# Pick 12 of every expert unit is gathered in two bounded halves

## The chip, the cores and the metric

The kernel runs on one core of a Trainium2 chip. The metric is the device time of one launch in microseconds (us). Engines are named as the profile names them: PE is TensorE (matrix products), PEld its weight loads, DVE is VectorE, ACT is ScalarE, POOL is GpSimd, SP is SyncE. POOL issues the indirect DMAs (gathers), SP the plain loads of weights. The gathers run on DMA queue q0, SP's loads on q1, and all queues share the core's 16 DMA engines.

## What is computed

The reference is a small model over 256 tokens of width 1024: two layers of attention with feed-forward blocks, then a state-space layer and a windowed attention layer, each followed by an expert layer ("peer") and a gated addition ("ple"). The change touches the two expert layers alone. Cut to what matters, one such layer is:

```
def peer_ffn(x, norm_g, q_w, sub_keys, u, v):
    h = rmsnorm(x, norm_g).reshape(T, D)                       # T = 256 tokens, D = 1024
    q = (h @ q_w).reshape(T, PEER_HEADS, 2, PEER_HALF)         # 8 heads
    s = einsum('thcd,ckd->thck', q, sub_keys)                  # 2 x 128 key scores per token and head
    s1, i1 = top_k(s[:, :, 0], 16)
    s2, i2 = top_k(s[:, :, 1], 16)
    ... the best 16 of the 256 sums s1 + s2; idx = i1 * 128 + i2, one of 16384 experts
    gate = softmax(best_s)
    a = einsum('nd,nhkd->nhk', h, u[idx])
    w = gate * gelu(a)
    out = einsum('nhk,nhkd->nd', w, v[idx])
```

So each token picks 16 experts per head, 128 in all, and for each of them a row of `u` and a row of `v` is fetched and used once.

## The kernel before

Everything is in 32-bit floats. The tokens are two blocks of 128, one token on each of 128 partitions. An expert's `u` and `v` rows lie side by side in one table in HBM, `experts`, of 2 x 16384 rows (both layers, one behind the other) of 2048 floats, which is 8 KB. One gather is one indirect DMA: it reads a row number from each partition and fetches that row, 128 rows or 1.05 MB in all.

**Units and picks.** A unit is one head of one token block: 16 units per layer (n = 0 to 15), 16 picks each (k = 0 to 15), so 256 gathers per layer and 512 in the kernel. Pick g of the kernel goes to buffer `held[g % 11]`; there are 11 buffers (`HELD`). Each buffer has its semaphore `expert_landed[g % 11]`, which a gather raises by 16 when it has landed.

**Who does what to a pick.** POOL waits until the buffer is free (`expert_free`, raised by PE after the pick that had the buffer before) and issues the gather (`gather` in `expert_rows`, L2840). DVE waits for the landing and multiplies the `u` half by the token's row, summing it to `a` (`dots`, L2723). ACT makes GELU, the weight, and a diagonal matrix of weights per pick (`weights`, L1903 to L1912). PE multiplies the diagonal with the `v` half in two products of 512 columns, each issued as more than one MATMUL record (`values`, L1300 and L1303), summing all picks of a block in PSUM. Picks are handled in order and in groups: 4 groups of 4 in units 0 to 14 (`EVEN`); in unit 15 (`FINE`) groups of two up to (12, 13), then 14 alone, then 15 alone. ACT starts on a group when DVE has finished all of its picks.

**What stands between.** In unit n DVE does, in this order: the dots of group 0, the gates, the top 16 keys of unit n+1 (`top_keys`, L2665 and on), the dots of group 1, the best pairs of unit n+1 (`top_pairs`), the dots of group 2, the expert numbers of unit n+1 (`experts_of`, L2179 to L2190), the dots of group 3. The last instruction of `experts_of_picks` (L2190) raises `peer_idx`, for which POOL waits before it issues pick 0 of unit n+1. In units 0 to 5, PE puts one more product of queries (L1258, with the key scores L1288) ahead of groups 0 and 2, and `top_keys` needs those scores, which ACT copies out (L1884).

**Behind the last unit.** When pick 255 is summed, DVE adds the result to the token rows (L2228), PE transposes them (L594) and works through the gate products of the ple layer (L695 to L697). The weight blocks of those products come by SP's loads; SP holds the fifth of them back until pick 253 of the layer (k = 13 of unit 15) has landed (`HELD_BACK`), and the others follow it.

Of the kernel before, what the change touches and what calls it, by code (L numbers as in the profile page):

```python
# [31 lines left out]
KEYS = 128  # L32
# [102 lines left out]
PICKS = UNITS * TOPK  # L135
HELD = 11
HELD_AT = 8088
SPACE = 31808
QUERY = {AT[f"peer{l}_q"] + m: (l, m) for l in range(2) for m in range(SUBS)}
NEXT_IN_RING = {AT[f"peer{l}_q"] + SUBS + i: AT[f"peer{l}_q"] + SLOTS + i for l in range(2) for i in range(RING)}  # L140
OUTS = {AT["ssm_out"]: 0, AT["swa_out"]: 1}
HELD_BACK = {AT[f"ple{l}_gate"] + 4: PICKS * (l + 1) - 3 for l in range(2)}
LAST_GATES = {AT[f"ple{l}_gate"] + 4 + i: PICKS * (l + 1) - HELD + i for l in range(2) for i in range(4)}
# [14 lines left out]
def build_program(nc, stream, experts, x_in, pos_in, cols_in, rows_in, out):  # L158
    n_blocks = AT["end"]
    ctx = ExitStack()  # L160
    with ctx:
# [149 lines left out]
        def peer_regions():  # L311
            r = places(ARENA, ("own", (2 * KEYS,)), ("s", (TB, SUBS, KEYS)), ("s2", (2, KEYS)), ("sv", (2, TOPK)),
                       ("si", (2, TOPK)), ("cand", (256,)), ("cand2", (256,)), ("bs", (TOPK,)),
                       ("bp", (TOPK,)), ("pa", (2, TOPK)), ("pf", (2, TOPK)), ("eq", (2, TOPK, TOPK)),
                       ("pk", (2, TOPK)), ("at", (TOPK,)), ("idx", (2, TOPK)), ("e", (2, TOPK)), ("sum", (1,)),
                       ("rc", (1,)), ("gate", (2, TOPK)), ("a", (2, TOPK)), ("g", (2, TOPK)), ("w", (2, TOPK)),
                       limit=HELD_AT)
            r["held"], _ = region(HELD_AT, HELD, EXPERT)
            r["q0"] = r["cand"]
            r["diag"] = split(row[:, 1, :], 2 * GROUP, P)  # L320
            r["qT"] = pick[:, 0:2, :]
            return r
# [191 lines left out]
        def _(sp):  # L514
# [6 lines left out]
            while b < n_blocks:  # L521
# [40 lines left out]
                    end += 1  # L562
                if b in HELD_BACK:
                    pick_of = HELD_BACK[b]
                    sp.wait_ge(expert_landed[pick_of % HELD], 16 * (pick_of // HELD + 1))
                first = b - RING + 1 if way == "used" else SPLIT[b - RING][2] + 1
                free = used if way == "used" else lo_ready[way]
                turns = (end - b) // RING
# [1454 lines left out]
        def _(dve):  # L2023
# [149 lines left out]
            def experts_of_picks(l, n, first, end):  # L2173

                R = peer_regions()
                si, bp, pa = R["si"].bitcast(U32), R["bp"].bitcast(U32)[:, first:end], R["pa"].bitcast(U32)
                wide, bits = (8, 3) if (first, end) == (0, 8) else (TOPK, 4)
                ks = slice(first, end)
                dve.tensor_scalar(pa[:, 0, ks], bp, bits, None, ALU.logical_shift_right)  # L2179
                link(dve.tensor_scalar(pa[:, 1, ks], bp, wide - 1, None, ALU.bitwise_and))  # L2180
                link(dve.tensor_copy(R["pf"][:, :, ks], pa[:, :, ks]))
                full = [P, 2, end - first, wide]
                eq = R["eq"][:, :, ks, 0:wide]
                iota = col("iota")[:, 0:wide].unsqueeze(1).unsqueeze(1).to_broadcast(full)
                link(dve.tensor_tensor(eq, R["pf"][:, :, ks].unsqueeze(3).to_broadcast(full), iota, ALU.is_equal))
                link(dve.tensor_tensor(eq, eq, si[:, :, 0:wide].unsqueeze(2).to_broadcast(full), ALU.mult))
                link(dve.tensor_reduce(R["pk"][:, :, ks].unsqueeze(3), eq, AX.X, ALU.add))
                link(dve.scalar_tensor_tensor(R["at"][:, ks], R["pk"][:, 0, ks], float(KEYS), R["pk"][:, 1, ks],
                                              ALU.mult, ALU.add))
                return dve.tensor_scalar(R["idx"].bitcast(U32)[:, n % 2, ks], R["at"][:, ks], float(KEYS * KEYS * l), None,  # L2190
                                         ALU.add)

            def add(n, y):

# [483 lines left out]
            def peer(l):  # L2678
# [38 lines left out]
                def dots(n, group):  # L2717
                    h = bank(4 + 2 * (n // PH), 2)
                    for k in range(*groups_of(n)[group]):
                        g = PICKS * l + TOPK * n + k  # L2720
                        u = R["held"][:, g % HELD, 0:D]
                        dve.wait_ge(expert_landed[g % HELD], 16 * (g // HELD + 1))
                        last = dve.scalar_tensor_tensor(u, u, 1.0, h, ALU.mult, ALU.mult,  # L2723
                                                        accum_out=R["a"][:, n % 2, k:k + 1])
                    last.then_inc(of("peer_a"), 1)
# [84 lines left out]
        def _(pool):  # L2810
# [19 lines left out]
            def expert_rows(l, at):  # L2830
                R = peer_regions()
                base = AT[f"peer{l}_q"]
                idx = R["idx"].bitcast(U32)

                def gather(n, ks):
                    for k in ks:
                        g = PICKS * l + TOPK * n + k
                        if g >= HELD:
                            pool.wait_ge(of("expert_free"), g - HELD + 1)
                        pool.indirect_dma_start(R["held"][:, g % HELD, :], None, experts,  # L2840
                                                bass.IndirectOffsetOnAxis(ap=idx[:, n % 2, k:k + 1], axis=0))\
                            .then_inc(expert_landed[g % HELD], 16)

                pool.wait_ge(of("peer_idx0"), l + 1)
# [182 lines left out]
```

## Time and profile before

| | |
|---|---|
| time, median of 3 runs | 2739.67 us (2739.56 to 2741.49) |
| span of the profiled execution | 2739.2 us |
| PE busy | 2461.3 us (90%) |
| DVE busy | 1915.0 us (70%) |
| ACT busy | 1178.3 us (43%) |
| POOL busy | 855.8 us (31%) |
| gathers (POOL DMA_INDIRECT) | 512, first issued at 1265.4 us, last at 2691.2 us |

The span runs from the first to the last instruction; the timed runs are 0.4 to 2.3 us above it. The busy shares are means over stages that have different limits: the two expert layers lie at about 1265 to 1930 us and 2050 to 2715 us, and the shares of the page say little of them. A row of the timeline has the start, the length, the engine, the line, the operation, output and inputs, and in brackets how long the engine was idle before it and who ended that.

### The profile page before, as it was taken

The page shows a single profiled execution, that of the slowest core. Times are in us where ns is not written, and L with a number is a line of the kernel's source. Part 1 is how long each engine was busy: PE and PEld are TensorE (multiplying, and loading weights), DVE is VectorE, ACT ScalarE, POOL GpSimd, SP SyncE. Part 2 cuts the span into 40 slices and gives each one's busy share as a digit, 9 for nine tenths or more (in the row PEclk, how much of TensorE's full clock was granted, in tenths as well). Part 3 has the DMA queues.
Part 4 walks back from the last instruction along what each step waited for, and adds up shares of the span by engine and source line. Part 5 has one row for each costly group of instructions (what it writes and reads, how often), then busy time and mean ns, then how long its engine had stood idle before and what let it go on. Part 6 is the DMA issues. An engine that isn't in the chain of part 4 may idle for free.

```text
span 2739.2 us, 32208 instructions
## 1 busy us (share of the span) xinstructions
PE 2461.3 (90%) x10416; PEld 1678.3 (61%) x10416; DVE 1915.0 (70%) x3841; ACT 1178.3 (43%) x2586; POOL 855.8 (31%) x700
## 2 busy tenths in 40 slices
PE   8999999999989999998998787789988998777688
PEld 7888788888778877986544333334765454333244
DVE  7885588888768875654676767666667676776675
ACT  4446744444564456563333333333453333323334
POOL 0005400000230026754333333444433333333442
PEclk9999999999999999999999889999999999999999
DMA  6654365556425553448999999999639999999996
GB/s 209 189 180 139 117 198 190 172 192 190 158 70 195 188 163 127 165 142 331 420 418 421 417 419 415 414 414 420 205 142 413 420 421 421 417 420 417 411 414 265
DMA packets 142240, 783.39 MB, mean 286 GB/s; under 512 B 15904, under 2 KB 16416, under 8 KB 76576
## 3 DMA queue, kind: packets, MB, share of 16 engines
q0 software_dynamic: 73728, 536.90, 47.4%
q1 hardware_dynamic: 65648, 237.45, 26.1%
q10 hardware_dynamic: 2736, 7.46, 0.9%
q8 instruction: 66, 1.08, 0.2%
q14 instruction: 62, 0.51, 0.1%
HBM read 780.69 MB, written 1.05 MB: 285 GB/s over the span
## 4 chain that ended last, share of the span: by engine, by line
PE 48%; DMA 22%; issue 9%; DVE 8%; ACT 7%; POOL 6%; another core or an unknown queue 0%; POOLq 0%; ACTq 0%; SPq 0%; DVEq 0%
DMA arena<-experts,arena 22%; PE ps L717 11%; PE ps L1300 6%; PE ps L1303 6%; PE ps L718 6%; PE ps L695 5%; PE ps L696 5%; PE ps L697 5%; POOL ring_lo L401 4%; DVE arena L2723 2%; ACT row L1912 2%; POOL arena L2840 1%; PE ps L1258 1%; ACT arena L1905 1%; ACT L1903 1%
## 5 line engine op out<-in xcount | busy, mean ns | idle before, releaser
L2723 DVE SCALAR_TENSOR_TENSOR arena<-arena,ps 128x1024 f32<-128x1024 f32 x512 | 616.4, 1219 | 370.3 <-DMA arena<-experts,arena 354.0
L1300 PE MATMUL ps<-arena,row 128*128 128x512 f32 x1024 | 568.3, 638 | 197.3 <-ACT row L1912 190.3
L2840 POOL DMA_INDIRECT arena<-experts,arena x512 | 485.3, 948 | 761.4 <-PE ps L1303 508.9
L1303 PE MATMUL ps<-arena,row 128*128 128x512 f32 x1024 | 549.7, 620 | 0.0
L717 PE MATMUL ps<-hT,ring_hi 128*128 128x512 f32 x1408 | 503.4, 400 | 2.9 <-DVE hT L2239 2.7
L394 ACT ACTIVATE ring_hi<-ring 128x1024 fp32r<-128x1024 f32 x408 | 429.8, 1058 | 172.4 <-PE ps L697 127.4
L1300 PEld LDWEIGHTS ps<-arena,row 128*128 128x128 f32 x1024 | 198.2, 202 | 474.5 <-ACT row L1912 259.5
L401 POOL TENSOR_TENSOR ring_lo<-ring,ring_hi 128x1024 fp32r<-128x1024 f32 x139 | 334.5, 2416 | 235.0 <-ACT ring_hi L394 212.7
L718 PE MATMUL ps<-hT,ring_lo 128*128 128x256 f32 x1408 | 395.9, 281 | 0.0
L1303 PEld LDWEIGHTS ps<-arena,row 128*128 128x128 f32 x1024 | 205.5, 201 | 266.4 <-issue 266.4
L401 DVE TENSOR_TENSOR ring_lo<-ring,ring_hi 128x1024 fp32r<-128x1024 f32 x269 | 324.1, 1228 | 18.3 <-ACT ring_hi L394 17.6
L717 PEld LDWEIGHTS ps<-hT,ring_hi 128*128 128x128 f32 x1408 | 265.3, 188 | 69.7 <-issue 3.1
L2817 POOL TENSOR_TENSOR rs<-ms,cols 128x1 f32<-128x1 f32 (+1 forms) x41 | 26.4, 645 | 842.2 <-DVE ms L2053 733.1
L718 PEld LDWEIGHTS ps<-hT,ring_lo 128*128 128x128 f32 x1408 | 266.7, 189 | 2.8
L1903 ACT ACTIVATE arena<-arena 128x4 f32<-128x4 f32 (+1 forms) x138 | 28.4, 206 | 533.2 <-DVE arena L2723 513.3
L1912 ACT ACTIVATE row<-cols,arena 128x128 f32<-128x128 f32 x512 | 164.6, 390 | 4.5
L695 PE MATMUL ps<-ring_hi,w 128*128 128x512 f32 x352 | 138.3, 393 | 3.0 <-DVE ring_lo L401 3.0
L1542 ACT ACTIVATE arena<-arena 128x256 f32<-128x256 f32 x88 | 36.9, 419 | 235.7 <-DVE arena L2280 235.7
L696 PE MATMUL ps<-ring_lo,w 128*128 128x512 f32 x352 | 137.9, 392 | 0.0
L697 PE MATMUL ps<-ring_hi,w 128*128 128x512 f32 x352 | 137.0, 389 | 0.0
L695 PE MATMUL ps<-hT,ring_hi 128*128 128x256 f32 (+1 forms) x392 | 114.1, 291 | 4.3 <-POOL ring_lo L401 2.4
L1905 ACT ACTIVATE arena<-arena 128x1 f32<-128x1 f32 x512 | 110.2, 284 | 4.5
(350 smaller groups left out, 3599.4 us busy)
## 6 DMA issues: line engine op xcount, KB each, us to landing
ring<-stream SPq DMA_DIRECT2D x424, 512.0 KB
arena<-experts,arena POOLq DMA_INDIRECT x512
row<-rows_in ACTq DMA_DIRECT2D x11, 512.0 KB, 5.2
arena<-stream SPq DMA_DIRECT2D x8, 512.0 KB, 5.8
queries_in_ring_hi<-stream SPq DMA_DIRECT2D x8, 512.0 KB
queries_in_w<-stream SPq DMA_DIRECT2D x4, 512.0 KB, 7.8
queries_in_h_lo<-stream SPq DMA_DIRECT2D x4, 512.0 KB, 5.3
x<-x_in SPq DMA_DIRECT2D x1, 1024.0 KB, 5.3
```

Source lines behind the costliest of these rows:

```text
L394: act.activation(part(b)[0], raw(b), ACT.Copy).then_inc(hi_ready, 1)
L401: e.tensor_tensor(lo, raw(b), hi.bitcast(F32), ALU.subtract).then_inc(lo_ready[who], 1)
L695: pe.matmul(dst, a[0], b[0], start=start, stop=False)
L696: pe.matmul(dst, a[0], b[1], start=False, stop=False)
L697: return pe.matmul(dst, a[1], b[0], start=False, stop=stop)
L717: pe.matmul(ps[:, bank_at, :], hi, hT[:, :, k, :], start=k == 0, stop=False)
L718: last = pe.matmul(ps[:, bank_at, 0:T], lo, hT_hi[:, k, :], start=False, stop=k == KD - 1)
L1300: lower = pe.matmul(ps[:, 2 * tb, :], diag, v[:, 0:HALF], start=first, stop=end)
L1303: pe.matmul(ps[:, 2 * tb + 1, :], diag, v[:, HALF:D], start=first, stop=end)\
L1912: last = act.activation(R["diag"][:, k % (2 * GROUP), :], col("ident"), ACT.Copy, scale=R["w"][:, n % 2, k:k + 1])
L2723: last = dve.scalar_tensor_tensor(u, u, 1.0, h, ALU.mult, ALU.mult, accum_out=R["a"][:, n % 2, k:k + 1])
L2840: pool.indirect_dma_start(R["held"][:, g % HELD, :], None, experts, bass.IndirectOffsetOnAxis(ap=idx[:, n % 2, k:k + 1], axis=0))\
```

## The change

Pick 12 of each unit is gathered by two indirect DMAs into its one buffer. The first takes the same row numbers as before, but has an upper bound, the last row of the lower half of the layer's table (8192 of 16384 rows); partitions whose number is above are left out. The second takes a second list of numbers, `upper`, in which a number of the lower half has been raised by 2^20, so that it is beyond its bound (the end of the table) and is left out. DVE makes that list with two more instructions on one column per unit. The second DMA is issued after pick 15 of the unit, and ahead of it POOL waits until the first has landed. Both raise the buffer's semaphore by 16, and `landed(g)` counts what to wait for.

```diff
+EXTRA_AT = HELD_AT + HELD * EXPERT
+IN_TWO = 12
+LOWER = 8192
+OUT_OF_RANGE = float(1 << 20)
...
+def landed(g):
+
+    return 16 * sum(1 + (h % TOPK == IN_TWO) for h in range(g % HELD, g + 1, HELD))
...
                     pick_of = HELD_BACK[b]
-                    sp.wait_ge(expert_landed[pick_of % HELD], 16 * (pick_of // HELD + 1))
+                    sp.wait_ge(expert_landed[pick_of % HELD], landed(pick_of))
...
-                return dve.tensor_scalar(R["idx"].bitcast(U32)[:, n % 2, ks], R["at"][:, ks], float(KEYS * KEYS * l), None,
-                                         ALU.add)
+                base = float(KEYS * KEYS * l)
+                if end == TOPK:
+                    late = slice(IN_TWO, IN_TWO + 1)
+                    link(dve.tensor_scalar(R["past"][:, late], R["at"][:, late], float(LOWER), OUT_OF_RANGE, ALU.is_lt, ALU.mult))
+                    dve.scalar_tensor_tensor(R["upper"].bitcast(U32)[:, n % 2, late], R["past"][:, late], base, R["at"][:, late],
+                                             ALU.add, ALU.add)
+                return dve.tensor_scalar(R["idx"].bitcast(U32)[:, n % 2, ks], R["at"][:, ks], base, None, ALU.add)
...
-                        dve.wait_ge(expert_landed[g % HELD], 16 * (g // HELD + 1))
+                        dve.wait_ge(expert_landed[g % HELD], landed(g))
...
+                        into = R["held"][:, g % HELD, :]
+                        if k != IN_TWO:
+                            pool.indirect_dma_start(into, None, experts,
+                                                    bass.IndirectOffsetOnAxis(ap=idx[:, n % 2, k:k + 1], axis=0))\
+                                .then_inc(expert_landed[g % HELD], 16)
+                            continue
+                        pool.indirect_dma_start(into, None, experts,
+                                                bass.IndirectOffsetOnAxis(ap=idx[:, n % 2, k:k + 1], axis=0),
+                                                bounds_check=KEYS * KEYS * l + LOWER - 1, oob_is_err=False)\
+                            .then_inc(expert_landed[g % HELD], 16)
+                    if IN_TWO in ks:
+                        g = PICKS * l + TOPK * n + IN_TWO
+                        pool.wait_ge(expert_landed[g % HELD], landed(g) - 16)
                         pool.indirect_dma_start(R["held"][:, g % HELD, :], None, experts,
-                                                bass.IndirectOffsetOnAxis(ap=idx[:, n % 2, k:k + 1], axis=0))\
+                                                bass.IndirectOffsetOnAxis(ap=upper[:, n % 2, IN_TWO:IN_TWO + 1], axis=0),
+                                                bounds_check=2 * KEYS * KEYS - 1, oob_is_err=False)\
                             .then_inc(expert_landed[g % HELD], 16)
```

On POOL, from the first gathers of the first expert layer to the start of unit 1, the program before has these rows (picks 0 to 7 and a small power, picks 8 to 10, picks 11 to 15, pick 0 of unit 1, the rest of unit 1):

```order
L2840 DMA arena<-experts,arena 128x2048 [waits blocks_used,peer_idx0]
L2840 DMA arena<-experts,arena 128x2048 x7
L2817 TENSOR_TENSOR rs<-ms,cols 128x1 [waits ms_ready]
L2840 DMA arena<-experts,arena 128x2048 [waits peer_idx]
L2840 DMA arena<-experts,arena 128x2048 x2
L2840 DMA arena<-experts,arena 128x2048 [waits expert_free] x5
L2840 DMA arena<-experts,arena 128x2048 [waits expert_free,peer_idx]
L2840 DMA arena<-experts,arena 128x2048 [waits expert_free] x15
```

The changed program has in the same place, from the small power on (L2864 is the bounded first gather of pick 12, L2871 the second):

```order
L2835 TENSOR_TENSOR rs<-ms,cols 128x1 [waits ms_ready]
L2860 DMA arena<-experts,arena 128x2048 [waits peer_idx]
L2860 DMA arena<-experts,arena 128x2048 x2
L2860 DMA arena<-experts,arena 128x2048 [waits expert_free]
L2864 DMA arena<-experts,arena 128x2048 [waits expert_free]
L2860 DMA arena<-experts,arena 128x2048 [waits expert_free] x3
L2871 DMA arena<-experts,arena 128x2048 [waits expert_landed1]
L2860 DMA arena<-experts,arena 128x2048 [waits expert_free,peer_idx]
L2860 DMA arena<-experts,arena 128x2048 [waits expert_free] x11
```

The second gather of pick 12 stands behind picks 13, 14 and 15, waits for the first to land, and pick 0 of the next unit stands behind it.

On DVE, in unit 0 of the first expert layer, the step that makes the expert numbers of unit 1 reads before, from the dot of pick 11 to that of pick 12:

```order
L2723 SCALAR_TENSOR_TENSOR arena<-arena,ps 128x1024 [waits expert_landed0]
L2179 TENSOR_SCALAR arena<-arena 128x16
L2180 TENSOR_SCALAR arena<-arena 128x16
L2181 CAST arena<-arena 128x32 [waits dve_chain]
L2185 TENSOR_TENSOR arena<-arena,cols 128x512 [waits dve_chain]
L2186 TENSOR_TENSOR arena<-arena 128x512 [waits dve_chain]
L2187 TENSOR_REDUCE arena<-arena 128x32 [waits dve_chain]
L2188 SCALAR_TENSOR_TENSOR arena<-arena 128x16 [waits dve_chain]
L2190 TENSOR_SCALAR arena<-arena 128x16 [waits dve_chain]
L2723 SCALAR_TENSOR_TENSOR arena<-arena,ps 128x1024 [waits expert_landed1]
```

and in the changed program its second half reads:

```order
L2200 TENSOR_REDUCE arena<-arena 128x32 [waits dve_chain]
L2201 SCALAR_TENSOR_TENSOR arena<-arena 128x16 [waits dve_chain]
L2206 TENSOR_SCALAR arena<-arena 128x1 [waits dve_chain]
L2207 SCALAR_TENSOR_TENSOR arena<-arena 128x1 [waits dve_chain]
L2209 TENSOR_SCALAR arena<-arena 128x16
L2741 SCALAR_TENSOR_TENSOR arena<-arena,ps 128x1024 [waits expert_landed1]
```

Two one-column instructions, L2206 and L2207, stand ahead of the one that releases POOL (L2209 now, L2190 before). The order of the dots is the same.

## Rows read from the trace of the kernel before

**Rows 1.** Page, part 3: DMA queue, kind: packets, MB, share of 16 engines.

```profile
q0 software_dynamic: 73728, 536.90, 47.4%
```

**Rows 2.** Windows: us; PE, PEld, DVE, ACT, POOL busy; clock; DMA share; GB/s.

```profile
1280.00:1915.00 635.00, 540.65 (x1332) 256.70 (x1330) 436.99 (x1068) 214.25 (x676) 246.61 (x253) 0.94 1.01 418
2070.00:2698.00 628.00, 527.86 (x1308) 249.64 (x1307) 434.97 (x1062) 212.81 (x670) 247.26 (x252) 0.95 1.01 417
```

**Rows 3.** Waits from 1280 to 1925 us: total, times, longest.

```profile
DVE arena L2723 <- DMA arena<-experts,arena: 183.2, 153, 2.6
...
POOL arena L2840 <- PE ps L1303: 256.8, 156, 14.0
POOL arena L2840 <- DVE arena L2190: 93.7, 14, 8.1
```

**Rows 4.** Timeline of POOL, units 3 and 4 of the first expert layer.

```profile
1421.83 0.94 POOL L2840 DMA_INDIRECT arena<-experts,arena  x1 [0.78 <-PE ps L1303]
1430.90 0.94 POOL L2840 DMA_INDIRECT arena<-experts,arena  x1 [8.14 <-DVE arena L2190]
```

**Rows 5.** Timeline of DVE, units 3 and 4 of the first expert layer.

```profile
1425.98 1.22 DVE L2723 SCALAR_TENSOR_TENSOR arena<-arena,ps 128x1024 f32<-128x1024 f32 x1 [1.26 <-DMA arena<-experts,arena]
...
1430.01 0.17 DVE L2190 TENSOR_SCALAR arena<-arena 128x16 uint32<-128x16 f32 x1
1430.10 1.21 DVE L2723 SCALAR_TENSOR_TENSOR arena<-arena,ps 128x1024 f32<-128x1024 f32 x1
...
1431.24 1.22 DVE L2723 SCALAR_TENSOR_TENSOR arena<-arena,ps 128x1024 f32<-128x1024 f32 x1
...
1435.91 1.22 DVE L2723 SCALAR_TENSOR_TENSOR arena<-arena,ps 128x1024 f32<-128x1024 f32 x1 [1.25 <-DMA arena<-experts,arena]
...
1438.40 1.22 DVE L2723 SCALAR_TENSOR_TENSOR arena<-arena,ps 128x1024 f32<-128x1024 f32 x1 [1.25 <-DMA arena<-experts,arena]
```

**Rows 6.** Timeline of ACT and DVE at the start of unit 3's key search.

```profile
1408.32 0.63 ACT L1884 ACTIVATE arena<-ps,rs 128x128 f32<-128x128 f32 x2 [7.84 <-PE ps L1288]
...
1408.97 0.49 DVE L2665 MAX8 arena<-arena 128x8 f32<-128x128 f32 x2 [1.97 <-ACT arena L1884]
```

**Rows 7.** Timeline of DVE, last picks (13, 14, 15) of the first expert layer.

```profile
1917.61 1.22 DVE L2723 SCALAR_TENSOR_TENSOR arena<-arena,ps 128x1024 f32<-128x1024 f32 x1 [1.26 <-DMA arena<-experts,arena]
...
1920.10 1.22 DVE L2723 SCALAR_TENSOR_TENSOR arena<-arena,ps 128x1024 f32<-128x1024 f32 x1 [1.25 <-DMA arena<-experts,arena]
...
1923.25 1.22 DVE L2723 SCALAR_TENSOR_TENSOR arena<-arena,ps 128x1024 f32<-128x1024 f32 x1 [1.92 <-DMA arena<-experts,arena]
```

**Rows 8.** Timeline of PE, last picks of the first expert layer.

```profile
1918.08 1.02 PE L1303 MATMUL ps<-arena,row 128*128 128x512 f32 x2
1920.37 1.13 PE L1300 MATMUL ps<-arena,row 128*128 128x512 f32 x2 [1.27 <-ACT row L1912]
...
1927.44 0.66 PE L594 MATMUL ps<-cols,x 128*128 128x128 f32 x4
```

**Rows 9.** Timeline, same place in the second expert layer (DVE: picks 13, 15).

```profile
2702.83 1.22 DVE L2723 SCALAR_TENSOR_TENSOR arena<-arena,ps 128x1024 f32<-128x1024 f32 x1 [2.23 <-DMA arena<-experts,arena]
...
2705.59 1.13 PE L1300 MATMUL ps<-arena,row 128*128 128x512 f32 x2 [2.24 <-ACT row L1912]
...
2708.42 1.22 DVE L2723 SCALAR_TENSOR_TENSOR arena<-arena,ps 128x1024 f32<-128x1024 f32 x1 [1.87 <-DMA arena<-experts,arena]
```

**Rows 10.** Timeline of PE in unit 13 of the first expert layer, after an idle stretch.

```profile
1812.11 1.02 PE L1303 MATMUL ps<-arena,row 128*128 128x512 f32 x2
1817.85 2.08 PE L1300 MATMUL ps<-arena,row 128*128 128x512 f32 x2 [4.72 <-ACT row L1912]
...
1824.13 1.02 PE L1300 MATMUL ps<-arena,row 128*128 128x512 f32 x2
```

**Rows 11.** Window inside that stretch, columns as in rows 2.

```profile
1818.00:1822.00 4.00, 4.00 (x5) 1.71 (x6) 2.40 (x6) 0.00 (x0) 0.09 (x1) 0.50 1.02 424
```

**Rows 12.** Timeline of SP, the held-back weight loads.

```profile
1917.61 41.45 SPq L579 DMA_DIRECT2D ring<-stream  x12
```

More of the change, by code:

```diff
@@ L318, in peer_regions @@
             r["held"], _ = region(HELD_AT, HELD, EXPERT)
+            r["upper"], at = region(EXTRA_AT, 2, TOPK)
+            r["past"], at = region(at, TOPK)
             r["q0"] = r["cand"]
@@ L2832, in expert_rows @@
                 base = AT[f"peer{l}_q"]
-                idx = R["idx"].bitcast(U32)
+                idx, upper = R["idx"].bitcast(U32), R["upper"].bitcast(U32)
                 def gather(n, ks):
```

## The prediction

> **What bounds the kernel now.** I read the page for the queues, then windows over the two gather stages, then the waits in them, then the timelines around one unit and around the last picks of a layer. The gathers bring 536.90 MB over q0 [rows 1], 512 of 1.05 MB each. In both stages the 16 DMA engines are busy all the time (share 1.01) and move 417 to 418 GB/s [rows 2], which is 2.5 us per gather. DVE, the first user of a pick, waits for landings 183.2 us in 153 places of the first stage [rows 3], and the dots of picks that it waits for start 2.49 us apart (1917.61, 1920.10) [rows 7]. So the rate of the DMA engines sets the length of a stage, as long as the queue never runs dry; POOL, DVE, ACT and PE have slack inside it. POOL's 256.8 us of waiting for PE and 93.7 us for L2190 [rows 3] are waiting for free buffers and for the next unit's numbers, with gathers queued meanwhile. How many: pick 15 of unit 3 is issued at 1421.83 and its dot starts at 1435.91, 14.1 us or five to six gathers later; pick 0 of unit 4 is issued at 1430.90 and used at 1438.40, 7.5 us or three gathers later [rows 4, 5]. The second is the thinnest point.
>
> At the end of a layer the bound changes: the last landing is followed by a chain through DVE, ACT and PE with nothing beside it. The dot of pick 13 starts at 1917.61 [rows 7], and the diagonals of the group (12, 13) let PE start at 1920.37, 2.76 us later. PE then works without a gap through picks 12 to 15 until the transposes at 1927.44 [rows 8]. The last dot, at 1923.25 [rows 7], is not in that chain, since pick 15's products stand behind three other picks'. The second layer repeats it (2702.83 to 2705.59, also 2.76 us; last dot at 2708.42) [rows 9].
>
> **Bytes and queue.** If left-out rows are not moved, each pick 12 still brings 128 rows, and the stage moves the same bytes. Thirty-two more indirect DMAs add only their own start and end. The rows show no fixed part per gather when the queue is full: 1.05 MB at 418 GB/s takes 2.51 us, the spacing of the dots 2.49 us. I take 0 for the 32. The other end is a left-out row that takes the time of a moved one: a second full gather per unit, 32 x 2.49 = 80 us. No row shows a bounded gather; I take the end where the row is simply absent.
>
> **The wait on POOL.** Behind it stand only pick 0 of the next unit and what follows. The first half of pick 12 lands before pick 13, and in unit 3 pick 11's dot starts at 1425.98 [rows 5]; half a gather later is 1427.2, a whole one 1428.5 at the worst division of the rows over the engines. POOL issues the second half then, 0.94 us, and is done by 1429.5, while the release for pick 0 comes with L2190 at 1430.01 and the issue at 1430.90 [rows 4, 5]. Picks 13 to 15 are in the queue meanwhile, 7.5 us of work. So the wait is covered by DVE's making of the numbers, at 0 us; a bounded gather could take about 1.4 us longer than 0.94 on POOL before it shows, and then pick 0 still has its own queue cover. That cover is 7.5 less its own transfer of 2.49, so at most 5.0 us, less whatever start the DMA needs; I take 2 us as safe. DVE's two instructions delay L2190 by 0.17 us each and a gap, 0.4 us together [rows 5]: 0 under that cover, 32 x 0.4 = 13 us without it.
>
> **The order of landing.** The second half of pick 12 is queued behind pick 15, so pick 12 is complete about when pick 15 was before. DVE takes dots in order, so in each unit the dots of 12 to 15 start together there. In unit 3 that is 1435.91 instead of 1430.10. At 1.14 us a dot (1430.10 to 1431.24) they end 4 x 1.14 later, 3.4 us after the end of pick 15's dot before. Next unit's picks come every 2.49 us from 1438.40 [rows 5], so DVE gains 1.35 us per pick and is level at its third. PE gets the group 3.4 us late and frees buffers 3.4 us late, which costs 1.4 of the five to six gathers queued there. In units 0 to 5 the lateness also reaches the key search, which already waits 1.97 us for scores made behind that group [rows 6]; it has the landing of four more picks, 10 us, to recover before the numbers are due. Inside the stage I put 0, with bounds of 0 and 2 us in each of the six such units of a layer, 24 us.
>
> **The end of a layer.** Here nothing covers the lateness. With the last bytes landing as before, the dot of pick 12 starts at 1923.25, that of 13 1.14 us later at 1924.39, and PE starts the group 2.76 us after that, at 1927.15 instead of 1920.37: 6.8 us later. In the second layer 2708.42 + 1.14 + 2.76 = 2712.32 instead of 2705.59: 6.7 us. PE then has the same four picks to do.
>
> Two things come on top. PE ends the group before at about 1919 [rows 8] and would now be idle for 8 us. After 4.72 us of idleness in unit 13 the next picks ran at a granted clock of 0.50, the level of 1.2 GHz [rows 10, 11]: from 1817.85 to 1824.13, 6.28 us, for eight MATMUL records that take 8 x 0.43 = 3.4 us at the pace of the layer's end (sixteen from 1920.37 to 1927.3) [rows 8]. So up to 2.8 us; the trace has shorter such stretches too, and I take 2.0. And SP's held-back loads start when pick 13 has landed (1917.61) [rows 12]; with only half of pick 12 ahead of it that is 1.2 us earlier, while more of the gathers is still to come. Before, the last dot came 3.15 instead of 2.49 us after the one ahead of it, 0.7 us of sharing; with half a gather more to share I take 0.5 us more. What follows the transposes is PE's own chain and moves as a whole.
>
> **Sum.** Per layer 6.8 + 2.0 + 0.5 = 9.3 us, two layers 18.6 us, inside the stages 0. Against the profiled span of 2739.2 that is 2757.8; the median of the runs shown is 0.5 above the span, so 2758.3 us, 0.7% slower. This case's own range is 2750 (no clock loss, no sharing, 2 x 6 us less a little) to 2768 (full clock loss, some of the units' bounds).
>
> **Rivals.**
> *Starved units.* The late group and the late numbers empty the queue in units 0 to 5. For it speaks the wait in [rows 6] and the three gathers of cover at pick 0; against it that four landings lie between. Up to 24 us more, or with 13 us for the DVE instructions 37 more: 2765 to 2795. Chance 0.15.
> *Left-out rows cost as moved ones, or a part of it.* Nothing in the trace speaks for or against; full price 80 + 18.6 makes 2838, half price 2798. Chance 0.06.
> *Each gather pays a fixed part.* If the engines finish one gather before the next, a half costs more than half. From the rows, the most that one can hide is the 5.0 us between issue and transfer of pick 0, 160 us for 32; against it stands the 2.49 us spacing, which leaves nothing. Should a fifth of it show, 2790. Chance 0.04. The Trainium skill, DMA: Bandwidth & Descriptors, on the anatomy of one DMA of the GpSimd path, puts a fixed cost of about 2.0 us on each DMA; by that, 32 more would be an estimated 64 us, were none overlapped. This trace does not show it between queued gathers (2.49 us apart).
> *POOL is slow on a bounded gather.* Sixty-four of them. Up to 2.3 us each nothing shows; at 10 us each, the excess over the cover of 3.4 us is 6 us in 30 units: 2930. Chance 0.04; a mild form falls in the first rival.
> *Not slower.* The end of a layer is set by the gate weights and not by PE: SP's loads start 1.2 us earlier, and if the gate products had to wait for them, PE's lateness would be hidden: 2737 to 2742. This decides only if those products now waited at least 9 us for weights, but PE goes from the last pick to the transposes without a stop [rows 8] and the loads start 10 us before. Chance 0.06.
>
> **Numbers.** The forecast has 0.65. Its 2758 is the prediction; 2747 to 2788 leaves out the costly left-out rows, slow POOL, fixed parts, the worst starvation and no change, about 0.2 together. A difference under 0.2% (5.5 us) cannot be told from none here. Slower is the forecast, the starved units and the three costly rivals, less a margin for a smaller end: 0.91. Same 0.06, faster 0.03.
>
> **What the profile would show.** Queue q0: the same megabytes, 32 x 16 more packets; more megabytes would be the second rival. In a unit, four dots of picks 12 to 15 back to back 1.14 us apart, after one wait for a landing, and POOL's L2871 issued ahead of the release by DVE. DMA share still 1.0 and the stages 635 and 628 us long within 2 us. At a layer's end, PE idle for some 8 us ahead of its last four picks and a granted clock of 0.5 behind that. Wrong would be the sum if the share fell inside the stages, if POOL's instruction grew past 2 us, or if the gates took up the lateness.

## The result and the profile after

The changed kernel takes 2766.32 us (median of 4 runs, 2765.81 to 2767.43), the kernel before on the same chip 2740.35 (4 runs, 2739.56 to 2741.49): ratio 1.0093, 95% interval 1.0082 to 1.0105, 26.0 us slower. The forecast was 18.6 us more than the profiled span and 2758 us in all; the time lies inside the range. The profiled span grew from 2739.2 to 2764.3 us, by 25.1.

First the page, part 1, part 3 (queue: packets, MB, share of 16 engines) and part 6 (issues, us to landing), of the kernel after:

```profile
span 2764.3 us, 32368 instructions
PE 2471.7 (89%) x10416; PEld 1681.3 (61%) x10416; DVE 1923.5 (70%) x3905; ACT 1177.1 (43%) x2586; POOL 892.8 (32%) x732
...
q0 software_dynamic: 78336, 536.92, 47.2%
...
HBM read 814.25 MB, written 1.05 MB: 295 GB/s over the span
...
arena<-experts,arena POOLq DMA_INDIRECT x544, 10.6
```

The queue carries the same megabytes as in [rows 1], with 4608 packets more: 512 for the 32 added DMAs (16 each) and 4096, which is one for each row left out (32 times 128). The counter of HBM reads was 780.69 MB before and is 33.56 MB higher, 4096 rows of 8 KB: it counts the rows left out in full. Whether the time does is for the experiments.

The windows of [rows 2], of the kernel after:

```profile
1280.00:1915.00 635.00, 525.61 (x1285) 248.20 (x1284) 440.61 (x1096) 212.14 (x669) 263.51 (x267) 0.93 1.01 415
2070.00:2698.00 628.00, 523.17 (x1270) 247.96 (x1270) 438.13 (x1103) 209.01 (x658) 263.15 (x267) 0.92 1.01 415
```

The DMA share is still 1.01, but the rate is 415 instead of 418 and 417 GB/s, 0.5 to 0.7% less: in 635 us some 3 to 5 us of gathers. So something was lost inside the stages too. The waits of the first stage (1280 to 1925 us; total, times, longest), of DVE and POOL:

```profile
DVE arena L2741 <- DMA arena<-experts,arena: 159.3, 86, 6.8
DVE arena L2683 <- ACT arena L1897: 25.4, 5, 6.1
...
POOL arena L2860 <- PE ps L1316: 243.9, 130, 9.3
POOL arena L2871 <- DMA arena<-experts,arena: 44.8, 12, 6.3
...
POOL arena L2860 <- DVE arena L2209: 23.3, 14, 2.6
```

POOL's wait for the next unit's numbers went from 93.7 us [rows 3] to 23.3, because POOL now stands at L2871 for most of that time. Grown is the second row: DVE's key search waits 25.4 us for the scores that ACT copies out. In the kernel before, the same view has for it:

```profile
DVE arena L2665 <- ACT arena L1884: 8.1, 4, 5.6
```

Around pick 0 of unit 4, the place of [rows 4, 5], the timelines of POOL and DVE after are:

```profile
1422.39 1.00 POOL L2864 DMA_INDIRECT arena<-experts,arena  x1 [1.31 <-PE ps L1316]
...
1429.66 1.50 POOL L2871 DMA_INDIRECT arena<-experts,arena  x1 [1.70 <-DMA arena<-experts,arena]
1432.67 0.94 POOL L2860 DMA_INDIRECT arena<-experts,arena  x1 [1.52 <-DVE arena L2209]
```

```profile
1431.97 0.15 DVE L2206 TENSOR_SCALAR arena<-arena 128x1 f32<-128x1 f32 x1
1432.15 0.16 DVE L2207 SCALAR_TENSOR_TENSOR arena<-arena 128x1 uint32<-128x1 f32 x1
1432.23 0.17 DVE L2209 TENSOR_SCALAR arena<-arena 128x16 uint32<-128x16 f32 x1
1438.50 1.22 DVE L2741 SCALAR_TENSOR_TENSOR arena<-arena,ps 128x1024 f32<-128x1024 f32 x1 [6.10 <-DMA arena<-experts,arena]
...
1439.65 1.22 DVE L2741 SCALAR_TENSOR_TENSOR arena<-arena,ps 128x1024 f32<-128x1024 f32 x1
...
1440.79 1.22 DVE L2741 SCALAR_TENSOR_TENSOR arena<-arena,ps 128x1024 f32<-128x1024 f32 x1
...
1441.93 1.22 DVE L2741 SCALAR_TENSOR_TENSOR arena<-arena,ps 128x1024 f32<-128x1024 f32 x1
```

L2871 is issued before the numbers are ready, and pick 0 still waits for DVE: the added wait is covered. The four dots of picks 12 to 15 run back to back behind one wait. Both are as forecast. L2209 comes 2.2 us later than L2190 did. Of that 0.8 us is the later start of the whole layer (its first gather is issued at 1266.21 instead of 1265.41), 1.2 the lateness of pick 11 of unit 3 counted from there, and 0.2 the two added instructions.

The end of the first layer, DVE (picks 11 to 13) and PE, the place of [rows 7, 8]:

```profile
1917.79 1.22 DVE L2741 SCALAR_TENSOR_TENSOR arena<-arena,ps 128x1024 f32<-128x1024 f32 x1 [1.25 <-DMA arena<-experts,arena]
...
1929.42 1.22 DVE L2741 SCALAR_TENSOR_TENSOR arena<-arena,ps 128x1024 f32<-128x1024 f32 x1 [10.41 <-DMA arena<-experts,arena]
...
1930.57 1.22 DVE L2741 SCALAR_TENSOR_TENSOR arena<-arena,ps 128x1024 f32<-128x1024 f32 x1
```

```profile
1927.92 1.02 PE L1316 MATMUL ps<-arena,row 128*128 128x512 f32 x2
1933.33 1.78 PE L1313 MATMUL ps<-arena,row 128*128 128x512 f32 x2 [4.38 <-ACT row L1925]
1934.90 1.91 PE L1316 MATMUL ps<-arena,row 128*128 128x512 f32 x2
1936.61 1.26 PE L1313 MATMUL ps<-arena,row 128*128 128x512 f32 x2
1937.70 1.02 PE L1316 MATMUL ps<-arena,row 128*128 128x512 f32 x2
...
1942.08 0.66 PE L607 MATMUL ps<-cols,x 128*128 128x128 f32 x4
```

From the dot of pick 13 to PE is 1933.33 - 1930.57 = 2.76 us, as before. PE's first six records then take 4.37 us (1933.33 to 1937.70), where 6 x 0.43 = 2.6 would do, and PE needs 8.75 us to the transposes where it needed 7.07 [rows 8]: 1.7 us for the clock. The window inside that stretch has a granted clock of 0.58, between the two levels, nearer to 1.2 GHz:

```profile
1933.00:1937.00 4.00, 3.67 (x5) 1.63 (x6) 1.08 (x2) 2.90 (x8) 0.89 (x1) 0.58 0.00 0
```

In the second layer PE's wait is 3.77 us, and the record behind it has the full pace (1.12 us, where layer 1 has 1.78):

```profile
2730.93 1.12 PE L1313 MATMUL ps<-arena,row 128*128 128x512 f32 x2 [3.77 <-ACT row L1925]
```

**Where the 25.1 us are.** I take each row's time from the first gather of its layer and set it against the same row of before. That gives four stretches: how late the dot of pick 11 of the last unit is (everything inside the stage), how much later the last landing and the dots of 12 and 13 let PE start, and PE's pace until the transposes.

| us later than before | layer 1 | layer 2 | forecast, a layer |
|---|---|---|---|
| pick 11 of unit 15 (inside the stage) | 4.4 | 3.7 | 0 |
| one dot, then 2.76 us to PE, behind the last landing | 6.8 | 6.7 | 6.8 |
| last landing further behind pick 11 | 1.0 | 0.4 | 0.5 |
| clock | 1.7 | 0.0 | 2.0 |
| PE at the transposes | 13.8 | 10.9 | 9.3 |

That is 24.8 of the 25.1 us. Each number is from one execution of each kernel; the same reading of e1 below, whose gathers are those of before, is up to 1.6 us off at the pick 11 of single units, and 0.4 and 0.1 us at that of unit 15. The third line is, in layer 1, (1929.42 - 1917.79) less what lay before between the dot of pick 11 (1912.64) and that of pick 15 (1923.25): 11.63 - 10.61. In layer 2 PE's pace did not fall. The end of the layer is near what was forecast (9.5 and 7.1 us, for 9.3); the 8.1 us of the first line were put at 0.

**How the late group makes pick 11 late.** Pick 11 of a unit goes into the buffer that pick 0 of the same unit had, so POOL can issue it only when PE has summed that pick 0. Here are its issue (POOL) and its dot (DVE) in unit 4 of layer 1, before:

```profile
1453.89 0.94 POOL L2840 DMA_INDIRECT arena<-experts,arena  x1 [5.92 <-PE ps L1303]
...
1465.73 1.22 DVE L2723 SCALAR_TENSOR_TENSOR arena<-arena,ps 128x1024 f32<-128x1024 f32 x1 [1.22 <-DMA arena<-experts,arena]
```

and after:

```profile
1461.54 0.94 POOL L2860 DMA_INDIRECT arena<-experts,arena  x1 [5.92 <-PE ps L1316]
...
1469.34 1.22 DVE L2741 SCALAR_TENSOR_TENSOR arena<-arena,ps 128x1024 f32<-128x1024 f32 x1
```

Counted from the layer's first gather, the issue is 6.8 us later, and the dot 2.8: before, 11.8 us lay between issue and dot, after 7.8. In units 3, 4 and 5 of layer 1 the issue is 4.4, 6.8 and 8.1 us late, and the time from issue to dot falls from 11.0, 11.8 and 12.8 us to 7.8 in each, so the dot is 1.2, 2.8 and 3.1 us late. The cover here was 3 to 5 us, and it is used up. Pick 0, in contrast, has more of it than before in unit 4 (10.4 us from issue to dot instead of 7.5). The windows from 1464 to 1472 us, before and then after, show that the queue runs short for a moment (share 1.01 and 0.95):

```profile
1464.00:1472.00 8.00, 8.00 (x31) 5.30 (x30) 6.57 (x15) 3.23 (x12) 1.49 (x2) 1.00 1.01 422
```

```profile
1464.00:1472.00 8.00, 8.00 (x20) 3.58 (x19) 7.79 (x21) 1.48 (x6) 4.59 (x5) 1.00 0.95 345
```

So what empties the queue is a buffer that PE frees late, and not the numbers of the next unit.

### The profile page after: what moved, and what is told of

Its sections match the earlier page's. It is cut to its first block, busy times and chain, and to the rows that moved or that the text cites. A ratio compares the mean times of both kernels' runs of the same rounds, so it can differ in the third digit from the quotient of the medians.

```text
span 2764.3 us, 32368 instructions
## 1 busy us (share of the span) xinstructions
PE 2471.7 (89%) x10416; PEld 1681.3 (61%) x10416; DVE 1923.5 (70%) x3905; ACT 1177.1 (43%) x2586; POOL 892.8 (32%) x732
## 3 DMA queue, kind: packets, MB, share of 16 engines
HBM read 814.25 MB, written 1.05 MB: 295 GB/s over the span
## 4 chain that ended last, share of the span: by engine, by line
PE 49%; DMA 21%; DVE 10%; issue 9%; ACT 6%; POOL 5%; POOLq 0%; ACTq 0%; SPq 0%; DVEq 0%
DMA arena<-experts,arena 21%; PE ps L730 11%; PE ps L1313 7%; PE ps L1316 6%; PE ps L731 5%; PE ps L708 5%; PE ps L709 5%; PE ps L710 5%; DVE arena L2741 4%; POOL ring_lo L414 4%; ACT row L1925 2%; ACT arena L1918 1%; ACT L1916 1%; DVE ring_lo L414 1%; DVE arena L2732 1%
## 5 line engine op out<-in xcount | busy, mean ns | idle before, releaser
L2741 DVE SCALAR_TENSOR_TENSOR arena<-arena,ps 128x1024 f32<-128x1024 f32 x512 | 604.5, 1218 | 343.6 <-DMA arena<-experts,arena 342.2
L1313 PE MATMUL ps<-arena,row 128*128 128x512 f32 x1024 | 579.0, 649 | 221.4 <-ACT row L1925 221.4
L2860 POOL DMA_INDIRECT arena<-experts,arena x480 | 453.5, 945 | 597.6 <-PE ps L1316 485.1
L1316 PE MATMUL ps<-arena,row 128*128 128x512 f32 x1024 | 557.2, 627 | 0.0
L1313 PEld LDWEIGHTS ps<-arena,row 128*128 128x128 f32 x1024 | 201.8, 205 | 500.2 <-ACT row L1925 286.0
L1316 PEld LDWEIGHTS ps<-arena,row 128*128 128x128 f32 x1024 | 208.9, 204 | 273.4 <-issue 273.4
```

Source lines behind the costliest of these rows:

```text
L1313: lower = pe.matmul(ps[:, 2 * tb, :], diag, v[:, 0:HALF], start=first, stop=end)
L1316: pe.matmul(ps[:, 2 * tb + 1, :], diag, v[:, HALF:D], start=first, stop=end)\
L2860: pool.indirect_dma_start(into, None, experts, bass.IndirectOffsetOnAxis(ap=idx[:, n % 2, k:k + 1], axis=0))\
```

## The experiments

The theory: landing order alone costs, at two places, the layer's end and the late group inside the stage. The rivals: the DVE instructions, the rows left out, the bounded gather itself, and the wait on POOL. All kernels compute the whole output. Each group of runs shared its runs of the kernel before: 2740.79 us for the first four, 2743.12 for the next four, 2743.49 for the last four; each ratio is against its own group. Where a kernel splits only some of the gathers, this helper replaces the test `k != IN_TWO`, and `landed` counts by it:

```
+def in_two(g):
+    n = g % PICKS // TOPK
+    return g % TOPK == IN_TWO and n == UNITS - 1
```

**e1, the numbers alone** (`n < 0`: the two DVE instructions stay, no gather is split).

> The kernel before with DVE's two instructions for the second list alone; no pick is split. Placing theory (the loss lies at a layer's end and in units 0 to 5, DVE's instructions are covered): 2740 us, within 1. Rival, late numbers: 0.4 us in each of 32 units, 2753.

Measured: 2740.28 us, ratio 0.9995 [0.9985, 1.0004]. The two instructions cost nothing that can be seen (interval -4.1 to +1.1 us).

**e2, the last unit alone** (`n == UNITS - 1`).

> Pick 12 is split in unit 15 of each layer alone. Placing theory: the layer's end is worth 3.4 us of late dots, 3 to 5 us of late and slower PE and about 1 us of queue per layer, 16 us in all: 2756. Rival, every split costs alike (26 us over 32): 2742.

Measured: 2761.77 us, ratio 1.0076 [1.0059, 1.0093], 21.0 us. Two split gathers of 32 (one in each layer) bring four fifths of the loss, 5 us more than the 16 that I expected for them. The timeline of PE at the end of its first layer:

```profile
1927.07 2.08 PE L1319 MATMUL ps<-arena,row 128*128 128x512 f32 x2 [9.37 <-ACT row L1931]
1928.94 1.91 PE L1322 MATMUL ps<-arena,row 128*128 128x512 f32 x2
1930.65 1.52 PE L1319 MATMUL ps<-arena,row 128*128 128x512 f32 x2
1932.00 1.02 PE L1322 MATMUL ps<-arena,row 128*128 128x512 f32 x2
```

PE is idle for 9.37 us (forecast: some 8) and then takes 4.93 us for six records, 2.4 us lost to the clock (forecast: 2.0).

**e3, all units but the last** (`n < UNITS - 1`).

> Pick 12 is split in units 0 to 14, and is whole in unit 15. Placing theory: 3 us per layer from a queue that runs short in the first units, 2746. Rival, every split costs alike: 30 of 32 remain, 2764.

Measured: 2751.59 us, ratio 1.0043 [1.0029, 1.0057], 10.8 us. Splits inside the stage do cost, not nothing as in the forecast, and more than the 6 us expected here. The sum with e2 is 31.8, more than the 26.0 of both together. The trace shows where: of e3's +4.7 us at the transposes of layer 1 only 1.5 are a late last dot. The rest is PE, which has a wait in unit 14,

```profile
1891.60 2.08 PE L1319 MATMUL ps<-arena,row 128*128 128x512 f32 x2 [4.91 <-ACT row L1931]
```

and no idle time from there to the transposes at 1932.17. In the kernel before PE had little idle time there: it was busy from 1880 to 1910 us, and waited for 0.17 and 1.27 us between 1910 us and the transposes. Its window (columns as in [rows 2]) of the kernel before:

```profile
1880.00:1910.00 30.00, 30.00 (x80) 14.90 (x79) 18.96 (x31) 11.54 (x37) 17.74 (x16) 0.98 1.01 420
```

So what PE loses to the late group of unit 14, beyond the little idle time that lay behind it, it carries to the end, unless it must wait there anyway, as in the full change.

**e4, the dot of pick 12 last.** The split stays everywhere; in units 0 to 14 DVE takes 13, 14 and 15 as they land, and 12 behind them.

```
-                    for k in range(*groups_of(n)[group]):
+                    picks = range(*groups_of(n)[group])
+                    for k in (13, 14, 15, 12) if picks == range(12, 16) else picks:
```

> As the changed kernel, but in units 0 to 14 DVE takes the dots of the last group in the order 13, 14, 15, 12, so that one dot and not four follows the late landing. If the late group starves the first units: 3 us per layer come back, 2760. If POOL's wait or the numbers do: no change, 2766.

Measured: 2761.86 us, ratio 1.0075 [1.0058, 1.0091], 21.1 us, which is e2's loss. Pick 11 of unit 15 is 0.8 us late in layer 1 and 1.5 in layer 2, where it was 4.4 and 3.7 in the changed kernel. In no unit does its dot start less than 10 us after its issue, and the window from 1464 to 1472 us has a share of 1.01 again. The waits of its first stage, columns as above:

```profile
DVE arena L2742 <- DMA arena<-experts,arena: 179.0, 154, 2.4
DVE arena L2683 <- ACT arena L1897: 5.2, 4, 2.4
```

With three of the four dots on time the key search waits 5.2 us, not 25.4. So the split gathers, the rows left out and the wait on POOL, all of them still there, cost next to nothing inside a stage (0.8 and 1.5 us here); the order of DVE's dots, and through it the time at which PE gets the group and frees its buffers, cost the rest.

**e5, e6 and e7, the stage in parts** (`n < 6`; `6 <= n < 13`; `13 <= n < 15`).

> Pick 12 is split in units 0 to 5 of each layer alone. Placing theory: here the key search waits behind the late group, so the queue runs short: 2 to 3 us per layer, 2745 (2743 to 2747). If the shortness is spread over all units: 2 us, 2742.

> Pick 12 is split in units 6 to 12 alone. Placing theory: PE has no queries or gates beside the picks there and catches up, the queue stays full: 2740, within 1.5. If every split costs alike (26 us over 32): 11 us, 2751.

> Pick 12 is split in units 13 and 14 alone. Theory from the run without unit 15: PE is full from unit 13 on (gate products beside the picks) and carries the late group of unit 14 to the layer's end, 3 us per layer: 2746. If the loss of that run came from the first units alone: 2740.

Measured: e5 2746.42, ratio 1.0012 [1.0002, 1.0021]; e6 2742.23, 0.9998 [0.9988, 1.0007]; e7 2748.08, 1.0019 [1.0009, 1.0028]. That is +3.3, -0.9 and +5.0 us; the interval of e5 starts at 0.5 us. The units between, in which PE makes no key scores ahead of the groups and which are far from the layer's end, are free. In the waits of its first stage, e5 has the same long stop of the key search as the changed kernel:

```profile
DVE arena L2689 <- ACT arena L1903: 25.6, 5, 6.0
```

In e5 the dot of pick 11 starts 7.8 us after its issue in units 3, 4 and 5 of both layers, in the changed kernel 7.8 to 8.3. In e2, e6 and e7, whose first units are not split, it takes 10 us or more there. In layer 1 of e5 pick 11 is 2.9 us late by unit 5, as in the changed kernel, but the last dot of the layer only 1.7 (layer 1) and -0.2 us (layer 2): where the later units are not split, part of the lateness is given back. By which slack, I did not settle, and the execution in the trace is the shortest of e5's ten (2742.30 us).

**e8, the first gather is whole.** It has no bound and moves all 128 rows; the second leaves all of them out.

```
-   ... R["past"][:, late], R["at"][:, late], float(LOWER), OUT_OF_RANGE, ALU.is_lt, ALU.mult
+   ... R["past"][:, late], R["at"][:, late], float(KEYS * KEYS), OUT_OF_RANGE, ALU.is_lt, ALU.mult
...
-                                               bass.IndirectOffsetOnAxis(ap=idx[:, n % 2, k:k + 1], axis=0),
-                                               bounds_check=KEYS * KEYS * l + LOWER - 1, oob_is_err=False)\
+                                               bass.IndirectOffsetOnAxis(ap=idx[:, n % 2, k:k + 1], axis=0))\
```

> As the changed kernel, but the first gather of pick 12 takes all 128 rows and the second leaves all 128 out; the order and the waits are the same, and so is the number of left-out rows. Order theory: the same landing of pick 12 behind pick 15, 2766 (2763 to 2768); the empty gather itself adds nothing. If the cost were in moving the second half of the rows late (1.2 us of transfer behind pick 15): up to 2.5 us less per layer, 2761.

Measured: 2767.26 us, ratio 1.0082 [1.0065, 1.0098], 24.1 us. It makes no difference how the bytes divide over the two gathers, nor that the second brings none. That leaves the order: DVE must wait for a DMA that is queued behind three others. The sharing with the held-back weights should have been less, with the whole pick moved early; the loss is not smaller beyond the interval. In its profiled execution, the longest of the four, layer 1 ends 11.2 us late and layer 2 15.9. The second number is 5.0 us more than in the changed kernel. Of these 2.9 come inside the stage: pick 11 is 5.4 us late in unit 5 (3.1 in the changed kernel) and 6.6 in unit 15 (3.7). The other 2.1 are PE's pace: after 6.66 us of idleness it takes 9.16 us to the transposes, where it took 7.06. Why the stage loses more there, I do not know.

**e9, empty gathers aside.** The kernel before, with 120 more gathers (one behind each group of units 1 to 15) that leave every row out, into a region that nobody reads.

```
+                        pool.indirect_dma_start(aside, None, experts.rearrange("e (h d) -> (e h) d", h=2),
+                                                bass.IndirectOffsetOnAxis(ap=nowhere[:, 0:1], axis=0),
+                                                bounds_check=4 * KEYS * KEYS - 1, oob_is_err=False)\
+                            .then_inc(of("aside_landed"), 16)
```

> The kernel before, no pick split, with four more gathers in each of units 1 to 15, one behind each group: all their numbers are beyond the bound, so all 128 rows (4 KB each) are left out; they go to unused space, and only the next of them waits for one. 15360 left-out rows, nearly four times those of the change. If a left-out row costs nothing on the DMA engines: 2742 (2739 to 2745). If it costs the reading that the page counts for it: 63 MB at 418 GB/s, 150 us more, 2890.

Measured: 2751.07 us, ratio 1.0028 [1.0017, 1.0039], 7.6 us, more than I expected. Over 120 gathers that is 0.06 us each (0.04 to 0.09 by the interval), with all that such a gather costs on POOL included. The page, part 3, of this kernel:

```profile
q0 software_dynamic: 91008, 536.97, 47.7%
...
HBM read 843.61 MB, written 1.05 MB: 307 GB/s over the span
```

The read counter rose by 62.9 MB, 15360 rows of 4 KB. At the 418 GB/s of [rows 2] such bytes would take 150 us; the kernel lost 7.6. So they are counted, and their time is not paid.

**e10, the wait with an empty queue.** The second half is issued right behind the first, ahead of pick 13, and POOL waits in between, inside its loop over the picks, with no gather behind the first half in the queue.

```
-                    if IN_TWO in ks:
-                        g = PICKS * l + TOPK * n + IN_TWO
                         pool.wait_ge(expert_landed[g % HELD], landed(g) - 16)
                         pool.indirect_dma_start(R["held"][:, g % HELD, :], None, experts,
...
```

> As the changed kernel, but the second half of pick 12 is issued before pick 13, so POOL waits for the first half with nothing queued behind it, and the order of landing is kept. If the three gathers between are what hides the wait: the queue idles about 4.5 us per unit (a half gather takes at least 5.9 us from issue to landing, 1.2 of it transfer), 2885 (2840 to 2920). If POOL's wait is harmless by itself: 2745.

Measured: 2957.88 us, ratio 1.0784 [1.0766, 1.0802], 214 us or 6.7 for each split, above the range that I gave. The timeline of POOL around one such place, and the window of its first stage (the profile names no releaser for this wait; it puts the other 31, 320.9 us, down to the DMA):

```profile
1440.62 1.00 POOL L2864 DMA_INDIRECT arena<-experts,arena  x1 [1.30 <-PE ps L1316]
1451.22 1.37 POOL L2869 DMA_INDIRECT arena<-experts,arena  x1 [9.60 <-issue]
```

```profile
1280.00:1915.00 635.00, 464.56 (x1106) 217.21 (x1105) 384.60 (x971) 181.34 (x574) 222.91 (x229) 0.88 0.89 360
```

The DMA share falls from 1.01 to 0.89: the engines do run dry. In this trace the second half, of about 64 rows, takes 4.4 to 6.2 us from issue to landing (median 5.0).

**e11, pick 14 in two** (`IN_TWO = 14`): the same program, but only pick 15 lies behind the first half in the queue.

> Pick 14 in place of pick 12 is split: one gather (15) stands between the halves, 2.5 us of cover. Cover theory: 4.7 - 2.5 = 2.2 us of idle queue per unit, and less lateness at the layer's end (two dots and PE from pick 14 on), 2815 (2780 to 2840). If only the order of landing counts: less than the changed kernel, about 2755.

Measured: 2876.10 us, ratio 1.0479 [1.0462, 1.0497], 133 us or 4.15 for each split, again above my range. 6.7 - 4.15 = 2.55 us is about one gather of cover, though the 4.15 also hold what the late landing of pick 14 costs, which no run separates. Its window has a share of 0.94:

```profile
1280.00:1915.00 635.00, 501.35 (x1186) 234.50 (x1184) 401.04 (x1022) 192.92 (x609) 238.10 (x245) 0.90 0.94 380
```

**e12, both cures**: split in units 0 to 14 alone, with the dots in the order 13, 14, 15, 12.

> Pick 12 is split in units 0 to 14, whole in unit 15, and the dots of the last group run 13, 14, 15, 12 there. Then neither a group nor a layer's end is late. If these two places are the whole loss: 2742 (2740 to 2745). If the first units' queue or PE at the end still lose: 2748.

Measured: 2744.44 us, ratio 1.0003 [0.9993, 1.0013]. Thirty of the 32 splits are there, and the loss is gone within the interval (-1.9 to +3.6 us). It is no gain either: splitting a gather brings nothing that this kernel lacks, and no version here beats the one before by more than its interval.

Not tried: the second half right behind the first without a wait. The two write different rows of one buffer, and DVE waits for both, so the order may not be needed; no run shows it.

## Why the prediction was right, and where its sum was short

**What bounds the kernel.** Right. The stages stayed bound by the DMA engines (share 1.01), and where they ran dry (e10, e11, and for moments in units 3 to 5) the time followed. The sign that I named, stages 635 and 628 us long within 2 us, did not hold: they grew by 4.4 and 3.7.

**Bytes and queue, at 0.** Right for the moved bytes, a little low for the rest. By e9 a gather with all its 128 rows left out costs 0.06 us; a split leaves out 128 rows in its two halves, so some 2 us in all, by that price. That fits e12 (+0.95 us) and the 0.8 and 1.5 us that stay inside the stages of e4. The Trainium skill, DMA: Bandwidth & Descriptors, Anatomy of one DMA, gives each DMA a fixed cost of about 2.0 us; in a full queue e9 shows 0.06 us of it. Where the queue is empty e10 shows 6.7 us, more than that figure. I read it so that the end of one gather, POOL's issue and the start of the next all lie open; no run takes the 6.7 us apart.

**The wait on POOL, at 0.** Right, and thinner than I wrote. POOL waited 95.9 us for the DMA at L2871 in all, and e4 and e12, which have such waits, lost next to nothing inside the stages. But e10 prices the wait at 6.7 us with no cover, e11 at 4.15 with one gather; by 2.5 us a gather the three of pick 12 cover 7.5, so by this estimate 0.8 us are to spare. I had reckoned with the wait's end on POOL and not with what the queue needs to start again.

**DVE's two instructions, at 0.** Right (e1).

**The order of landing inside the stage, at 0.** This is the step that failed: it measured 4.4 and 3.7 us, 8.1 together. I wrote that PE "frees buffers 3.4 us late, which costs 1.4 of the five to six gathers queued there", and took pick 0 for the thinnest point. The five to six were read at pick 15. Pick 11, which waits for PE as well, had only 3 to 5 us of cover in units 3 to 5, and its buffer came free 4.4 to 8.1 us late: more than 3.4. As I read it, the late group also holds up the key search (25.4 us of waiting instead of 8.1) and with it the next groups. So pick 11 is 1.2 us late in unit 3, 2.8 in unit 4 and 3.1 in unit 5 of layer 1, and about 3 until unit 14. I had also argued that the key search "has the landing of four more picks, 10 us, to recover before the numbers are due". The numbers were indeed not the trouble, since pick 0 kept its cover; the buffers were. The bound that I kept beside the 0, up to 2 us in each of six units, was wide enough for the true size of 3 to 4 us a layer. e4 takes the loss away by the order of dots alone, and e5, with splits in units 0 to 5 alone, has the same short stay of pick 11 in the queue and a loss of 3.3 us (0.5 to 5.8) in both layers together. Why that is less than 8.1, though e6 costs nothing, is not shown. The last 1.4 us of layer 1 come between unit 14 and pick 11 of unit 15, where POOL waits 6.22 us for PE ahead of pick 7; my text had nothing of it, and no run separates it.

**The end of a layer.** Right: the order of the dots costs 6.8 and 6.7 us as worked out. The clock was put at 2.0 for each layer and was 1.7 and 0. PE was idle 4.38 us in layer 1 and 3.77 in layer 2, not 8, since it was still busy with what the stage had left it; e2, where nothing is late inside, has the 8 (9.37 and 2.4 us of clock). That layer 2 lost nothing to the clock, where 2.0 us were forecast, is luck for the sum: it hides a part of the term put at 0. SP's loads started (1921.84) 4.05 us behind the dot of pick 11 instead of 4.97 (1917.61 [rows 12] less 1912.64), 0.9 us earlier (forecast 1.2), and the last landing came 1.0 and 0.4 us later (forecast 0.5).

**The rivals.** Starved units was no rival but a part: a mild form of it, 8 us of the 24 that it could have been, went on top of the forecast, by late buffers and not by late numbers. Left-out rows at a price: 0.06 us, not 2.5. A fixed part: hidden in a full queue. A slow bounded gather: 1.00 us on POOL for the first half, 1.10 at the median for the second, against 0.94. Not slower: PE had no wait for weights that could hide its lateness.

## What to carry to other kernels

When a user takes its buffers in order, split work costs by where its last piece stands in the queue, and not by its bytes: ask of each piece who waits for it next, which buffers that waiter frees, and how much is queued where those buffers are wanted. The cover has to be read at every place where the issuing engine waits, not at one. A group at the end of a stage has no next group to hide behind, so leave the last one whole. Inside the stage, letting the late member be used last was enough; at the end it was not tried. And a wait of the issuing engine for its own transfer is free only as long as enough is queued behind it: here three gathers of 2.5 us were enough, one (4.15 us lost) and none (6.7 us lost) were not, and two were not tried.

## What the runs showed of the hardware

- A row that a bounded indirect DMA leaves out is still one packet on the queue, and is counted in full as an HBM read (+33.56 MB for 4096 rows of 8 KB, +62.9 MB for 15360 of 4 KB), but costs almost no time: 7.6 us for 120 gathers of 128 such rows. The counter is no measure here of the time on the DMA engines.
- To wait for a gather to land before the next is issued, with none queued behind it, cost the kernel 6.7 us each time (e10), where 1.05 MB in a full queue takes 2.5.
- PE's idleness before its last picks was followed by a granted clock of 0.58 in layer 1 (after 4.38 us) and by full pace in layer 2 (after 3.77 us). In the kernel before, 2.79 us of it (up to 1857.62 us) were followed by half the pace, so its length alone does not tell.
